# Two items earlier: the order of a grouped hi/lo pipeline in the value half of an expert layer, on one Trainium2 core

## The chip, the cores and the metric

One NeuronCore of one Trainium2 chip runs the whole program in one launch. The metric is the device time of the kernel in microseconds (us), from its runs on the chip. TensorE is named PE in the profile, VectorE DVE, ScalarE ACT, GpSimd POOL, SyncE SP; PEld is TensorE's weight load. The granted clock of TensorE is given as a share of 2.4 GHz.

## The reference, cut to what matters

The program is one step of a hybrid decoder layer: a mixer (SSD and RG-LRU heads), an expert layer with product keys (PEER), and a closing with a per-layer embedding. 544 tokens (512 of a prompt, 8 x 4 decoded) of width 1024 pass through it. The change lies in the expert layer and in preparations for the closing:

```python
u = expert_u[idx]                                            # 16384 experts, 8 heads, top 16
act = jax.nn.gelu(jnp.einsum('td,thkd->thk', tb, u))
v = expert_v[idx]
return jnp.einsum('thk,thkd->td', g * act, v)
...
g = jax.nn.sigmoid(rmsnorm(h, lw['norm_ple_gate']) @ lw['w_ple_gate'])
h = h + rmsnorm((p @ lw['w_ple_proj']) * g, lw['norm_ple_out'])
```

For 384 of the tokens the kernel computes this densely: activations of all 16384 experts (128 blocks of 128), multiplied by a matrix of gates that is zero where an expert was not chosen, times all of expert_v. For the other 160 tokens it gathers the rows of the chosen experts.

## The kernel before, in words

**Stages.** Each engine runs one long program of its own; order between engines comes from semaphores alone. The expert stage (`experts`, from L1424 on) is a loop over 272 items n: n = 0 to 143 (NIT = 144) are the query and U half, n = 144 to 271 (NALL = 272) the V half. V item g = n - 144 (0 to 127) is one block of 128 experts: its slice of expert_v, 128 x 1024, is the weight of 24 matmuls with 384 columns (`v_item`, L1579), three for each of 8 PSUM banks: high weight by high activation (L1587), high weight by low activation (L1588), low weight by high activation (L1589). This splitting of fp32 into a high and a low part in fp32r is done for every operand.

**The ring** (`Ring`, L152 to L170). The weights go through three buffers of four slots. SP loads Rw(m), once ScalarE and VectorE have done with the slot's last item (m - 4); ScalarE rounds it to Rh(m) when TensorE has finished item m - 4; VectorE makes Rl(m) = Rw(m) - Rh(m). Both work four items ahead: at item n they make Rh(n + 4) and Rl(n + 4).

**The groups.** The other operand is made for four items at a time, for group i (items 4i to 4i + 3), in three steps:

- `h_full(i)` (L1958 to L1964, VectorE): Aq = Aq x Gq, the activations times the gates, 128 x 1536. It waits for the loads of Aq(i) and Gq(i // 2).
- `h_hi(i)` (L1720 to L1723, ScalarE): Hh = Aq rounded. It waits for h_full(i) and until TensorE has finished group i - 2, whose buffer it takes.
- `h_lo(i)` (L1966 to L1968, VectorE): Hl = Aq - Hh, counted in semaphore hlo. TensorE waits for it at the group's first item.

Aq has three buffers, Gq, Hh and Hl two each. In each engine's program these steps have fixed places: in VectorE's step for item g with g % 4 = 0 stands h_full(g // 4 + 1), in that with g % 4 = 2 h_lo(g // 4 + 1), in ScalarE's with g % 4 = 1 h_hi(g // 4 + 1). Each step first does the ring's own part, which waits for the end of item g, so that a step runs after its item. Group 0 is made in the last steps of the U half.

**SP's queue** (`sync`, L1460 to L1516). For item m it loads Rw(m). Where m - 151 is 2 modulo 4 it then loads for group i, four groups on, Gq(i // 2) if i is even (`load_g`, L1487, 1.5 MB, waits until h_full has used the buffer) and Aq(i) (`load_a`, L1480, 0.75 MB, waits for `hlo` >= i - 2). A wait on SP holds all loads behind it. All of them use one queue, q1; the gathers of GpSimd use q0.

**The gathered rows** (`row`, L1971; L1976 and L1981). GpSimd gathers 320 times 128 rows of 4 KB (512 KB) into four buffers, at most three ahead of VectorE. VectorE consumes them at a fixed pace, 1.4 per item in the V half, in its step for the item, after the ring's part and the group's.

**First halves of the closing.** `closing` needs the high and low parts of three tensors: the embedding (128 x 1088), its projection (128 x 2048) and the first slice of a gate matrix (128 x 1024). `early_scalar` (L2110 to L2118) rounds all three in a row in ScalarE's step for item 244 (g = 100), `early_vector` (L2120 to L2128) subtracts all three in a row in VectorE's step for item 245. Their loads are issued much earlier (m = 214).

Of the kernel before, what the change touches and what calls it, by code (L numbers as in the profile page):

```python
# [1380 lines left out]
def experts(nc, sh, ring, keys, vn, un, early):  # L1381
# [48 lines left out]
    TURN = 77  # L1430
    G0 = 79
    GEND = 139

    def need(e, name, v):

# [28 lines left out]
    def rows(n):  # L1464

        return range(rows_upto(n - 1), rows_upto(n))
# [200 lines left out]
    def scalar(a):  # L1667
        a.wait_ge(S("sq_free"), 4 * ND)
        a.activation(halves(rstd[:, :]), pair(3), ACT.Sqrt, scale=1.0 / D, bias=sh.epsc[:, 0:1]).then_inc(S("root"), 1)
        a.preload_act_table(ACT.Gelu_apprx_tanh)  # L1670

        def q_out(n, i):
            a.wait_ge(S("wmm"), n + 1)
            need(a, "scm", i - 1)
            a.copy(halves(qT[:, i % 2, :]), pair(1)).then_inc(S("qev"), 1)

        def u_out(n, g):
            if n < NR:
                a.wait_ge(S("evac"), 3 * NXC + g + 1)
                a.activation(Ab[:, g, :], Ab[:, g, :], ACT.Gelu_apprx_tanh).then_inc(S("glu"), 1)  # L1680
                return
            a.wait_ge(S("wmm"), n + 1)
            need(a, "as%d" % (g % 4), 16 * (g // 4))
            a.activation(Ab[:, g % 4, :], PS[:, g % 2, 0:DT], ACT.Gelu_apprx_tanh).then_inc(S("glu"), 1)  # L1684

        def score_out(hd):
            q, r = hd // 4, slice(32 * (hd % 4), 32 * (hd % 4) + 32)
            for s in range(2):
                a.wait_ge(S("scm"), 2 * hd + s + 1)
                need(a, "tkd", hd - 1)  # L1690
                a.copy(tk[:, hd % 2, :, s, :], PS[:, 4 + 2 * s, :].rearrange("p (b k) -> p b k", b=NDB)
                       ).then_inc(S("tkc"), 1)
                a.copy(tkS[r, q, s, :], PS[r, 5 + 2 * s, 0:PK]).then_inc(S("tkc"), 1)

        def turn_out(b):
            a.wait_ge(S("gtp"), b + 1)
            a.copy(ijg[:, :, b * P:(b + 1) * P], PS[:, 4 + b, 0:3 * P].rearrange("p (q t) -> p q t", q=3)
                   ).then_inc(S("gtc"), 1)
            a.mul(ijn[:, b * P:(b + 1) * P], PS[:, 4 + b, 2 * P:3 * P], -2.0).then_inc(S("gtn"), 1)

        def one_hot_act(j):
            t = 4 * j + 3
            a.wait_ge(S("gtc"), t // P + 1)
            a.wait_ge(S("gtn"), t // P + 1)
            need(a, "gmm", j - 3)
            a.activation(Asq[:, j % 2, :], iota[:, :], ACT.Square, scale=-1.0, bias=ijg[:, 0, t:t + 1]
                         ).then_inc(S("gaa"), 1)
            a.wait_ge(S("gaa"), 2 * j + 1)
            a.activation(Aoh[:, j % 4, 3, :], Asq[:, j % 2, :], ACT.Relu, scale=ijn[:, t:t + 1],
                         bias=ijg[:, 2, t:t + 1]).then_inc(S("gaa"), 1)  # L1710

        def gate_out(j):
            b = j // 8
            a.wait_ge(S("gmm"), j + 1)
            if j % 8 == 0 and b >= 2:
                a.wait_ge(S("gw%d" % (b % 2)), 16 * (b // 2))
            a.copy(stg[:, b % 2, :, 4 * (j % 8):4 * (j % 8) + 4].rearrange("p i t -> p t i"),
                   PS[:, 2 + j % 2, :].rearrange("p (t i) -> p t i", t=4)).then_inc(S("gev"), 1)

        def h_hi(i):  # L1720
            a.wait_ge(S("hfd"), i + 1)
            need(a, "wmm", VI + 4 * (i - 1) if i >= 2 else 0)
            a.copy(Hh[:, i % 2, :, :], Aq[:, i % 3, :, :]).then_inc(S("hhi"), 1)  # L1723

        def exps(g):
            a.preload_act_table(ACT.Exp)
            a.wait_ge(S("smx"), g + 1)
            a.activation(tu[:, 4, :], tu[:, 4, :], ACT.Exp).then_inc(S("cf"), 1)
            a.preload_act_table(ACT.Gelu_apprx_tanh)

        a.wait_ge(S("out_s"), 16 * 3)
        for n in range(NIT):
            if n >= NR and u_of(n) is None:
                q_out(n, QITEM.index(n))
            if n >= NR and u_of(n) is not None:
                u_out(n, u_of(n))
            ring.hi(a, n + 4)
            if n < 4:
                for k in (2 * n, 2 * n + 1):
                    a.wait_ge(S("normed"), 2 * ND + k + 1)  # L1740
                    a.copy(Xh[:, k, :], xf[:, k, :]).then_inc(S("xs"), 1)
            if n < NR and u_of(n) is not None:
                u_out(n, u_of(n))
            if n == NR + 2:
                for s, dst in enumerate((xtok, xtokS)):
                    a.wait_ge(S("xt"), s + 1)
                    for q in range(2):
                        a.copy(dst[:, q * 512:(q + 1) * 512], PS[:, 4 + 2 * s + q, :]).then_inc(S("xtc"), 1)
            if head_at(n, 4) is not None:
                score_out(head_at(n, 4))  # L1750
            if n in (LOOK[0] + 1, LOOK[1] + 1):
                exps(LOOK.index(n - 1))
            if n == TURN + 1:
                for b in range(NDB - 1):
                    turn_out(b)
            for j in units(n + 1):
                one_hot_act(j)
            for j in units(n):
                gate_out(j)
            if n == NIT - 1:  # L1760
                h_hi(0)
        for n in range(NIT, NALL):
            if n + 4 < NALL:
                ring.hi(a, n + 4)
            if n == NIT + 100:
                early[1](a)
            g = n - VI
            if g % 4 == 1 and g // 4 + 1 < PK // 4:
                h_hi(g // 4 + 1)
            if rows_upto(n) >= IDC > rows_upto(n - 1):  # L1770
                a.wait_ge(S("sdt"), IDC)
                a.activation(coef[:, :], dots[:, :], ACT.Gelu_apprx_tanh).then_inc(S("cf"), 1)

    def vector(v):
# [183 lines left out]
        def h_full(i):  # L1958
            v.wait_ge(S("aq%d" % (i % 3)), 16 * (i // 3 + 1))
            v.wait_ge(S("gq%d" % ((i // 2) % 2)), 16 * (i // 4 + 1))  # L1960
            v.tensor_tensor(Aq[:, i % 3, :, :].rearrange("p i (b t) -> p i b t", b=NGB),
                            Aq[:, i % 3, :, :].rearrange("p i (b t) -> p i b t", b=NGB),
                            Gq[(i // 2) % 2][:, :, (i % 2) * 4 * GTK:(i % 2 + 1) * 4 * GTK]
                            .rearrange("p b (i t) -> p i b t", i=4), ALU.mult).then_inc(S("hfd"), 1)  # L1964

        def h_lo(i):  # L1966
            v.wait_ge(S("hhi"), i + 1)
            v.tensor_tensor(Hl[:, i % 2, :, :], Aq[:, i % 3, :, :], Hh[:, i % 2, :, :].bitcast(F32), ALU.subtract  # L1968
                            ).then_inc(S("hlo"), 1)
# [15 lines left out]
        for n in range(NALL):  # L1985
# [39 lines left out]
                    one_hot_b(j // 2)  # L2025
                one_hot_a(j)
            g = n - VI
            if n == NIT + 101:
                early[2](v)
            if n == NIT - 2:  # L2030
                h_full(0)
            if n == NIT - 1:
                h_lo(0)
            if g >= 0 and g % 4 == 0 and g // 4 + 1 < PK // 4:
                h_full(g // 4 + 1)
            if g >= 0 and g % 4 == 2 and g // 4 + 1 < PK // 4:
                h_lo(g // 4 + 1)
            for r in rows(n):
                if r == IDC:
                    v.wait_ge(S("cf"), 3)  # L2040
                    v.tensor_tensor(coef[:, :], coef[:, :], gd[:, :], ALU.mult).then_inc(S("cf"), 1)
                    v.wait_ge(S("cf"), 4)
                row(r)
# [11 lines left out]
def closing(nc, sh, pT, w_plg, w_plp, y):  # L2055
# [51 lines left out]
        sp.dma_start(wpr[:, :, :], w_plp).then_inc(S("ple_in"), 16)  # L2107
        sp.dma_start(Wr[0][:, :, :], w_plg[0, :, :, :]).then_inc(S("wp0"), 16)

    def early_scalar(a):  # L2110

        a.wait_ge(S("wmm"), NIT)
        a.wait_ge(S("gmm"), NU)
        a.wait_ge(S("ple_in"), 32)
        a.copy(phi[:, :, :], praw[:, :, :]).then_inc(S("cwhi"), 1)
        a.copy(wph[:, :, :], wpr[:, :, :]).then_inc(S("cwhi"), 1)
        a.wait_ge(S("wp0"), 16)
        a.copy(Wh[0][:, :, :], Wr[0][:, :, :]).then_inc(S("cwhi"), 1)  # L2118

    def early_vector(v):  # L2120

        v.wait_ge(S("cwhi"), 1)
        v.tensor_tensor(plo[:, :, :], praw[:, :, :], phi[:, :, :].bitcast(F32), ALU.subtract).then_inc(S("cwlo"), 1)
        v.wait_ge(S("cwhi"), 2)
        v.tensor_tensor(wpl[:, :, :], wpr[:, :, :], wph[:, :, :].bitcast(F32), ALU.subtract).then_inc(S("cwlo"), 1)
        v.wait_ge(S("cwhi"), 3)
        v.tensor_tensor(Wl[0][:, :, :], Wr[0][:, :, :], Wh[0][:, :, :].bitcast(F32), ALU.subtract
                        ).then_inc(S("cwlo"), 1)  # L2128

    def sync(sp):  # L2130
        sp.wait_ge(S("sdt"), 2 * IDC)
# [357 lines left out]
```

## Time and profile before

| | us |
|---|---|
| median of 3 runs | 1865.39 |
| lowest, highest | 1860.92, 1871.02 |
| profiled execution: span, first to last instruction | 1857.5 |
| lines 1587 to 1589, first to last start (V half) | 1189.6 to 1767.9 |
| TensorE busy in the span | 1774.4 (96%) |
| VectorE busy | 1517.1 (82%) |
| mean granted clock of TensorE | 0.986 |

For the profiled execution the profile gives its span; a time of its own beside the span is not given, and the median of the runs lies 7.9 us above the span. The page of the profile lists busy times of the engines, the costliest groups of instructions and the chain that ended last; the list of waits says which instruction's arrival ended an engine's idle time; windows give busy time, granted clock, DMA share and GB/s of a stretch. Times of instructions are in us from the start of the span.

### The profile page before, as it was taken

How to read it: one execution, taken by the hardware profiler on the slowest of the kernel's cores; microseconds unless marked ns; L12 is line 12 of the kernel's file. 1: busy time of each engine (PE TensorE's matmuls, PEld its weight loads, DVE VectorE, ACT ScalarE, POOL GpSimd, SP SyncE). 2: the span in 40 equal slices, each digit the busy share in tenths (PEclk: the TensorE clock that was granted, in tenths of full speed). 3: DMA queues.
4: the chain of work that ended last, by engine and by line, in shares of the span. 5: the costliest groups of instructions: out<-in, count | busy, mean ns of one | idle time of the engine just before them, and what ended most of it. 6: DMA issues, size and time to landing. Idle time of an engine off the chain costs nothing.

```text
span 1857.5 us, 29685 instructions
## 1 busy us (share of the span) xinstructions
PE 1774.4 (96%) x11346; PEld 1713.3 (92%) x11346; DVE 1517.1 (82%) x2749; ACT 837.9 (45%) x1206; POOL 514.7 (28%) x415
## 2 busy tenths in 40 slices
PE   7999999999999999999999999699999999989996
PEld 6999986789999999999999999699999999989995
DVE  7748896867668689999999989578888888888777
ACT  5556652334334233357777777223333333332263
POOL 3100210000000012344444344344444444444300
PEclk9999999999999999999999999799999999999998
DMA  4222342134335456789999999999999999999511
GB/s 160 83 68 80 132 140 80 63 125 169 123 122 168 169 168 237 264 311 369 366 373 352 362 358 356 379 370 383 368 369 385 388 385 385 371 333 339 204 57 49
DMA packets 164124, 462.82 MB, mean 249 GB/s; under 512 B 16944, under 2 KB 77040, under 8 KB 161296
## 3 DMA queue, kind: packets, MB, share of 16 engines
q1 hardware_dynamic: 117904, 293.13, 44.1%
q0 software_dynamic: 46080, 167.79, 24.1%
q8 instruction: 91, 1.49, 0.3%
q14 instruction: 49, 0.40, 0.1%
HBM read 405.53 MB, written 55.34 MB: 248 GB/s over the span
## 4 chain that ended last, share of the span: by engine, by line
PE 70%; DVE 13%; DMA 11%; ACT 3%; issue 3%; SPq 0%; POOL 0%; DVEq 0%; ACTq 0%
PE PS L470 12%; PE PS L1574 8%; PE PS L1575 8%; PE PS L1576 8%; DMA Rw<-vn 7%; PE PS L1587 5%; PE PS L1589 5%; PE PS L1588 5%; PE PS L1557 5%; PE PS L1644 5%; PE PS L2177 2%; DVE Hl L1968 2%; DMA ug<-vn,idxU 2%; DVE Rl L170 1%; ACT Rh L165 1%
## 5 line engine op out<-in xcount | busy, mean ns | idle before, releaser
L165 ACT CAST Rh<-Rw 128x1024 fp32r<-128x1024 f32 x272 | 284.4, 1046 | 400.8 <-PE PS L1589 338.7
L170 DVE TENSOR_TENSOR Rl<-Rw,Rh 128x1024 fp32r<-128x1024 f32 x272 | 332.5, 1223 | 145.6 <-ACT Rh L165 139.1
L1587 PE MATMUL PS<-Hh,Rh 128*128 128x384 f32 x1024 | 349.4, 341 | 43.7 <-DVE Hl L1968 42.9
L1533 POOL DMA_INDIRECT ug<-un,idxU x160 | 239.3, 1495 | 540.5 <-DVE dots L1976 356.8
L1574 PE MATMUL PS<-Xh,Rh 128*128 128x384 f32 x992 | 342.8, 346 | 3.8 <-DVE Rl L170 2.8
L1589 PE MATMUL PS<-Hh,Rl 128*128 128x384 f32 x1024 | 346.2, 338 | 0.0
L1588 PE MATMUL PS<-Hl,Rh 128*128 128x384 f32 x1024 | 346.0, 338 | 0.0
L1575 PE MATMUL PS<-Xl,Rh 128*128 128x384 f32 x992 | 334.2, 337 | 0.0
L1576 PE MATMUL PS<-Xh,Rl 128*128 128x384 f32 x992 | 333.4, 336 | 0.0
L1533 POOL DMA_INDIRECT ug<-vn,idxU x160 | 230.5, 1441 | 282.3 <-DVE yacc L1981 217.4
L1587 PEld LDWEIGHTS PS<-Hh,Rh 128*128 128x128 f32 x1024 | 195.3, 191 | 53.2 <-issue 53.0
L1588 PEld LDWEIGHTS PS<-Hl,Rh 128*128 128x128 f32 x1024 | 195.3, 191 | 0.0
L1589 PEld LDWEIGHTS PS<-Hh,Rl 128*128 128x128 f32 x1024 | 194.9, 190 | 0.0
L1574 PEld LDWEIGHTS PS<-Xh,Rh 128*128 128x128 f32 x992 | 186.6, 188 | 7.1 <-DVE Rl L170 4.6
L1575 PEld LDWEIGHTS PS<-Xl,Rh 128*128 128x128 f32 x992 | 186.6, 188 | 0.0
L1576 PEld LDWEIGHTS PS<-Xh,Rl 128*128 128x128 f32 x992 | 186.2, 188 | 0.0
L1684 ACT ACTIVATE Ab<-PS 128x384 f32<-128x384 f32 x124 | 60.9, 491 | 255.2 <-PE PS L1576 252.6
L1981 DVE SCALAR_TENSOR_TENSOR yacc<-ug,coef,yacc 128x1024 f32<-128x1024 f32 x128 | 164.6, 1286 | 9.2 <-DMA ug<-vn,idxU 6.0
L1976 DVE CUSTOM_DVE_ANT_0 ug<-ug,xtok 128x1024 f32<-128x1024 f32 x128 | 154.1, 1221 | 19.9 <-DMA ug<-un,idxU 19.6
L470 PE MATMUL PS<-xhi,Whi 128*128 128x272 f32 (+1 forms) x560 | 119.3, 294 | 10.6 <-DVE xlo L913 9.0
L674 ACT CAST Whi<-Wr 128x1024 fp32r<-128x1024 f32 x51 | 53.3, 1044 | 150.6 <-PE PS L470 142.8
L470 PE MATMUL PS<-xhi,Wlo 128*128 128x272 f32 (+1 forms) x560 | 116.6, 290 | 0.0
(438 smaller groups left out, 3150.3 us busy)
## 6 DMA issues: line engine op xcount, KB each, us to landing
Rw<-uw SPq DMA_DIRECT2D x144, 512.0 KB
Rw<-vn SPq DMA_DIRECT2D x128, 512.0 KB
Wr<-wm SPq DMA_DIRECT2D x51, 512.0 KB, 3.3
acts<-Ab SPq DMA_DIRECT2D x128, 192.0 KB
gates<-stg SPq DMA_DIRECT2D x12, 2048.0 KB
Gq<-gates SPq DMA_DIRECT2D x16, 1536.0 KB
Aq<-acts SPq DMA_DIRECT2D x32, 768.0 KB
L<-acsd SPq DMA_DIRECT2D x4, 1024.0 KB, 6.9
```

Of the source, the lines that this page charges most:

```text
L165: a.copy(self.Rh[:, q, :], self.Rw[:, q, :]).then_inc(self.S("rhi"), 1)
L170: v.tensor_tensor(self.Rl[:, q, :], self.Rw[:, q, :], self.Rh[:, q, :].bitcast(F32), ALU.subtract).then_inc(self.S("rlo"), 1)
L470: r = pe.matmul(pair(b, m)[:, q, :], w_sb[:, s, k, 0:m], x_sb[:, k, q * HT:(q + 1) * HT], start=first, stop=last)
L1533: p.indirect_dma_start(out=ug[:, r % 4, :], out_offset=None, in_=un if r < IDC else vn, in_offset=bass.IndirectOffsetOnAxis(ap=idxU[:, r % ...
L1574: pe.matmul(out, Rh[:, q, w], x_hi[:, k, P:NP], start=(k == 0), stop=False)
L1575: pe.matmul(out, Rh[:, q, w], x_lo[:, k, P:NP], start=False, stop=False)
L1576: r = pe.matmul(out, Rl[:, q, w], x_hi[:, k, P:NP], start=False, stop=(k == ND - 1))
L1587: pe.matmul(out, Rh[:, q, w], hh, start=(g == 0), stop=False)
L1588: pe.matmul(out, Rh[:, q, w], hl, start=False, stop=False)
L1589: r = pe.matmul(out, Rl[:, q, w], hh, start=False, stop=(g == PK - 1))
L1976: v.tensor_tensor_reduce(ug[:, q, :], ug[:, q, :], (xtok if own else xtokS)[:, :], 1.0, 0.0, ALU.mult, ALU.add, dots[:, c:c + 1]).then_inc ...
L1981: v.scalar_tensor_tensor(out=y[:, :], in0=ug[:, q, :], scalar=coef[:, c:c + 1], in1=y[:, :], op0=ALU.mult, op1=ALU.add).then_inc(S("sdt"), 1)
```

## The change

Steps of a group move by two items. h_full(i), h_hi(i) and h_lo(i) stand two items earlier in their engines' programs: h_full for group g // 4 + 2 at g % 4 = 2, h_hi for group g // 4 + 2 at g % 4 = 3, h_lo for group g // 4 + 1 at g % 4 = 0. For group 1 this means that h_full(1) runs in VectorE's step for item 142, ahead of h_lo(0), and h_hi(1) right after h_hi(0). The three first halves of the closing are made one by one: on ScalarE in the steps for items 241, 245 and 249, on VectorE in those for 242, 246 and 250. SP's program, TensorE's and GpSimd's are the same.

```diff
+    EARLY = [NIT + 97, NIT + 101, NIT + 105]
...
             if n == NIT - 1:
                 h_hi(0)
+                h_hi(1)
         for n in range(NIT, NALL):
             if n + 4 < NALL:
                 ring.hi(a, n + 4)
-            if n == NIT + 100:
-                early[1](a)
+            if n in EARLY:
+                early[1](a, EARLY.index(n))
             g = n - VI
-            if g % 4 == 1 and g // 4 + 1 < PK // 4:
-                h_hi(g // 4 + 1)
+            if g % 4 == 3 and g // 4 + 2 < PK // 4:
+                h_hi(g // 4 + 2)
...
             g = n - VI
-            if n == NIT + 101:
-                early[2](v)
+            if n - 1 in EARLY:
+                early[2](v, EARLY.index(n - 1))
             if n == NIT - 2:
                 h_full(0)
             if n == NIT - 1:
                 h_lo(0)
             if g >= 0 and g % 4 == 0 and g // 4 + 1 < PK // 4:
-                h_full(g // 4 + 1)
-            if g >= 0 and g % 4 == 2 and g // 4 + 1 < PK // 4:
                 h_lo(g // 4 + 1)
+            if g >= -2 and g % 4 == 2 and g // 4 + 2 < PK // 4:
+                h_full(g // 4 + 2)
...
+    def early_scalar(a, part):
+        if part == 0:
+            a.wait_ge(S("wmm"), NIT)
+            a.wait_ge(S("gmm"), NU)
+            a.wait_ge(S("ple_in"), 32)
+            a.copy(phi[:, :, :], praw[:, :, :]).then_inc(S("cwhi"), 1)
+        elif part == 1:
+            a.copy(wph[:, :, :], wpr[:, :, :]).then_inc(S("cwhi"), 1)
+        else:
+            a.wait_ge(S("wp0"), 16)
+            a.copy(Wh[0][:, :, :], Wr[0][:, :, :]).then_inc(S("cwhi"), 1)
...
+    def early_vector(v, part):
+        v.wait_ge(S("cwhi"), part + 1)
```

`early_vector` is divided in the same way, into its three subtractions.

## Rows read from the trace of the kernel before

**Rows 1.** Page, busy time of the engines, share of the span, instructions.
```profile
PE 1774.4 (96%) x11346; PEld 1713.3 (92%) x11346; DVE 1517.1 (82%) x2749; ACT 837.9 (45%) x1206; POOL 514.7 (28%) x415
```

**Rows 2.** Waits, 1180 to 1775 us: engine, line, releaser; total, times, longest.
```profile
ACT Rh L165 <- DMA Rw<-vn: 45.8, 16, 4.4
PE PS L1587 <- DVE Hl L1968: 42.9, 18, 17.5
...
DVE yacc L1981 <- DMA ug<-vn,idxU: 6.0, 9, 1.2
```

**Rows 3.** Windows by stretch (A, B, C): busy, granted clock, DMA share, GB/s.
```profile
1189.57:1228.09 38.52, 36.26 (x192) 35.67 (x193) 26.61 (x32) 11.20 (x10) 14.25 (x11) 0.93 1.03 381
1228.09:1658.26 430.17, 408.64 (x2304) 401.68 (x2305) 364.73 (x290) 138.07 (x124) 195.21 (x135) 0.99 1.00 375
1658.26:1768.25 109.99, 107.62 (x601) 105.89 (x602) 84.59 (x70) 27.98 (x25) 38.66 (x28) 0.96 0.73 267
```

**Rows 4.** Timeline of DVE and PE around 1422 us; window of items 53 and 54.
```profile
1421.22 1.75 DVE L1968 TENSOR_TENSOR Hl<-Aq,Hh 128x1536 fp32r<-128x1536 f32 x1
...
1422.72 0.34 PE L1589 MATMUL PS<-Hh,Rl 128*128 128x384 f32 x1
1423.12 0.41 PE L1587 MATMUL PS<-Hh,Rh 128*128 128x384 f32 x1
...
1427.36:1435.67 8.31, 8.31 (x49) 8.31 (x49) 6.87 (x6) 3.49 (x3) 2.44 (x2) 1.00 1.05 396
```

**Rows 5.** Chain of waits, 1327 to 1337 us: start, us, what.
```profile
1317.66 14.48 DMA Rw<-vn
...
1332.16 1.06 ACT Rh L165
...
1333.29 1.11 issue
1334.39 1.76 DVE Hl L1968
...
1336.29 0.41 PE PS L1587
```

**Rows 6.** Waits on SP's queue, 1190 to 1770 us.
```profile
SPq L1484 <- DVE Hl L1968: 147.2, 28, 9.1
```

**Rows 7.** Windows with full queues, and of two groups without a listed stall.
```profile
1423.12:1457.07 33.95, 33.80 (x193) 33.22 (x193) 29.77 (x24) 11.19 (x10) 16.08 (x11) 1.00 1.02 383
...
1369.50:1405.50 36.00, 34.35 (x196) 33.53 (x194) 31.20 (x25) 11.19 (x10) 16.23 (x11) 1.00 1.04 394
1477.50:1513.50 36.00, 33.90 (x185) 33.29 (x184) 27.27 (x22) 10.12 (x9) 14.74 (x11) 0.95 1.03 397
1513.50:1549.50 36.00, 34.45 (x196) 33.90 (x197) 31.31 (x25) 12.22 (x11) 16.19 (x11) 1.00 1.02 382
```

**Rows 8.** Timeline of the closing's first halves on DVE, and PE after them.
```profile
1648.10 1.29 DVE L2123 TENSOR_TENSOR ple_lo<-ple_raw,ple_hi 128x1088 fp32r<-128x1088 f32 x1
1649.30 2.29 DVE L2125 TENSOR_TENSOR wp_lo<-wp_raw,wp_hi 128x2048 fp32r<-128x2048 f32 x1
...
1658.26 0.66 PE L1587 MATMUL PS<-Hh,Rh 128*128 128x384 f32 x1 [4.71 <-DVE Hl L1968]
```

**Rows 9.** The entry: chain of waits, timeline of DVE and PE, one window.
```profile
1168.52 14.02 DMA Aq<-acts
...
1182.57 1.76 DVE L1961 TENSOR_TENSOR Aq<-Aq,Gq 128x1536 f32<-128x1536 f32 x1 [9.38 <-DMA Aq<-acts]
...
1189.57 0.66 PE L1587 MATMUL PS<-Hh,Rh 128*128 128x384 f32 x1 [17.51 <-DVE Hl L1968]
...
1182.00:1188.00 6.00, 0.00 (x0) 0.00 (x0) 5.43 (x7) 1.47 (x1) 1.96 (x2) 0.50 1.05 395
```

**Rows 10.** DMA queues from 1210 to 1216 us: packets, MB, share.
```profile
q1 hardware_dynamic: 1680, 1.84, 93.4%
q0 software_dynamic: 97, 0.33, 14.2%
```

More of the change, by code:

```diff
@@ L2108, in early_sync @@
         sp.dma_start(Wr[0][:, :, :], w_plg[0, :, :, :]).then_inc(S("wp0"), 16)
[L2110 to L2128, printed above, removed]
+    def early_scalar(a, part):
[11 more added lines that the diff above has]
+        v.wait_ge(S("cwhi"), part + 1)
+        if part == 0:
+            v.tensor_tensor(plo[:, :, :], praw[:, :, :], phi[:, :, :].bitcast(F32), ALU.subtract
+                            ).then_inc(S("cwlo"), 1)
+        elif part == 1:
+            v.tensor_tensor(wpl[:, :, :], wpr[:, :, :], wph[:, :, :].bitcast(F32), ALU.subtract
+                            ).then_inc(S("cwlo"), 1)
+        else:
+            v.tensor_tensor(Wl[0][:, :, :], Wr[0][:, :, :], Wh[0][:, :, :].bitcast(F32), ALU.subtract
+                            ).then_inc(S("cwlo"), 1)
     def sync(sp):
```

## Prediction

> **What bounds the kernel now.** I read the page first: TensorE is busy for 1774.4 of 1857.5 us [rows 1], so only its own waits can be won. The list of waits says where they lie in the V half: 42.9 us before L1587 on VectorE's Hl, 18 times [rows 2]. The longest, 17.51 us, is the one before V item 0; the other 17 make 25.4 us. The windows by stretch [rows 3] cut the half into A (items 0 to 7, 38.52 us), B (items 8 to 103, 430.17 us) and C (items 104 to 127, 109.99 us).
>
> The reader is to see next that every fourth item waits, even where no stall is listed. In a quiet group Hl runs from 1421.22 for 1.75 us; the last matmul of the item before starts at 1422.72, and its successor not 0.17 us later but at 1423.12, 0.15 us after Hl's end [rows 4]. Inside a group two items take 8.31 us, 4.155 each [rows 4]. So TensorE alone would need 96 x 4.155 = 398.9 us for B, and B takes 31.3 us more.
>
> The chain of waits shows why Hl is late [rows 5]: an Rw load issued at 1317.66 lands after 14.48 us, ScalarE rounds it, VectorE makes Rl, only then comes h_lo in VectorE's order, and TensorE starts at 1336.29, 2.73 us late. In the old order h_lo(i) stands after item 2 of a group and is wanted at the end of item 3. From the end of an item, the hi cast (1.06), Rl (1.11 to its end as the chain shows it) and Hl (1.76) are 3.9 us; with semaphores that is one item, and the slack is nil. SP's queue closes a loop: load_a waits for Hl for 147.2 us in 28 places, 5.3 us each [rows 6], and the ring's loads stand behind it.
>
> The DMA columns say what comes next. Over B the DMA share is already 1.00 at 375 GB/s [rows 3]; the share can pass 1 a little, since packets overlap.
>
> **The change part by part.** No instruction is added or removed. In 31 groups h_full, h_hi and h_lo (1.75 us an Hl [rows 4], and as many elements each) run two items earlier, in the same total of 364.73 us of VectorE in B's 430.17 [rows 3].
>
> *h_lo earlier.* It ends about 4 us after item 0 of the group before and is wanted three items later, 12.5 us: slack 8.5 us in place of none. The largest listed stall inside the loop, 2.73 us, is covered three times. What TensorE waits for next is Rl(m) itself, made four items ahead: three items after its cast may start, so it has about the same 8.5 to 10 us of slack.
>
> *DMAs that move.* load_g stays where it is; it waits only for h_full. load_a(i) is written at the same place but its wait for Hl is now met when SP comes to it, so it goes straight after load_g instead of some 5.3 us later, and the ring's loads behind it are not held. From load_a's issue to h_full(i) there are nine items both before and after. For load_g the distance falls from eleven items to nine, 37 us, against landings of 14 us [rows 5]: covered. The exception is the entry (below).
>
> *h_full and h_hi earlier.* They need Aq and Gq landed, see above. h_hi(i) needs the last item of group i-2 done, which the ring's own cast in the same step already waits for: nothing.
>
> *B: what the freed time is worth.* Here the shares decide. The bytes are fixed: 375 GB/s x 430.17 us = 161.3 MB. At TensorE's 398.9 us that would be 404 GB/s. The three fullest windows of 36 us reached 394, 397 and 382 at shares of 1.02 to 1.04 [rows 7], mean 391. I take 391, as those are windows in which the queues were never empty, which is what the change brings: 161.3 / 0.391 = 412.6 us, a gain of 17.6. Bounds: 383, the rate of two groups that ran without a listed stall [rows 7], gives 421.2 us (gain 9.0); 397 gives 406.3 (gain 23.9). The Trainium skill (HBM Reference, Specifications (TRN2)) gives 358 GB/s as a core's share and about 425 for a core that streams alone. By the first B would take 450 us, more than it does, so the trace refutes it here; by the second B would be TensorE's alone.
>
> *A.* 38.52 us at 381 GB/s is 37.5 at 391: gain 1.0 (0 to 2.6: TensorE alone needs 8 x 4.155 = 33.2 us, and 0.07 x 38.5 = 2.7 for the clock of 0.93 after the entry [rows 3]).
>
> *C, with the closing's first halves.* The three casts and, from 1648.10, the three subtractions each ran in one piece and delayed Hl: 4.71 us of idle TensorE, then matmuls from 0.66 us at its lower level, 1.2 GHz [rows 8]; the granted clock of 0.96 over C is worth 0.04 x 110 = 4.4 us [rows 3]. Now the pieces stand four items apart, the largest 2.29 us on VectorE. In such a step VectorE has Rl 1.1, this 2.3, h_full 1.8 and one or two gathered rows at 1.2 (364.73 us of B less 96 Rl of 1.2 and 48 group steps of 1.75 leave 165 us for 135 gathers [rows 3]): up to 7.6 us against 4.2, hidden by the 8.5 us of slack and by lighter steps around it. Without that cover it would cost 3 us once. C needs 24 x 4.155 = 99.7 us, 10.3 below now; its DMA share is 0.73, so DMA does not bound it as a whole. I take 9, since the last A and G loads fall in its first third (bounds 7, the stall and half of the clock's part, and 10.3).
>
> *The entry.* h_full(1) and h_hi(1) now come before h_lo(0). h_full(0) starts at 1182.57, when Aq(0) has landed after 14.02 us, and TensorE starts at 1189.57, after Hl(0) [rows 9]. h_full(1) puts some 1.7 us between them, and waits for Aq(1), issued right behind. From 1182 to 1188 DMA moved 2.37 MB (6 us at 395 GB/s [rows 9]), three loads of 0.79 MB: Aq(1) landed by 1188 at the latest. Cost 1.7 to 5.5 us; I take 2.7, for one load of 0.79 MB needs 2 us after Aq(0) and VectorE comes to it after 1.7.
>
> **Sum:** -1.0 - 17.6 - 9.0 + 2.7 = -24.9 us against the profiled span of 1857.5, so 1832.6. The median of the runs, 1865.39, lies 7.9 above that span; with it unchanged the forecast is 1840.5 us.
>
> **The rivals.** *TensorE alone bounds it:* -2.6, -31.3, -10.3, +1.7 are -42.5: 1822.9 us. For it: waits for Rw leave 8.5 us of slack. Against: it needs 404 GB/s where the best window shows 397. The skill's 425 GB/s would lead here.
>
> *DMA is already the bound:* the share of 1.00 is saturation, and TensorE's stalls only change their name, from Hl to Rl. For it: 45.8 us of ScalarE's idle time, in 16 places, is on the Rw load [rows 2], and every Rw on the chain takes about 14 us. Then B gives 0 to 9, C 7, the entry costs 4: 3 to 12 us, 1853 to 1862. Against: the mean of B is 1.00 and its fullest window 1.04 [rows 3, 7]; the difference is time in which the queues ran dry.
>
> *Starved gathers (slower):* Gq and Aq now go out as one burst of 2.36 MB, 15 times. While such a burst ran, from 1210 to 1216, queue 1 had 93.4% and the gathers' queue 14.2% [rows 10]. A row that isn't there stops VectorE in row(), and behind it stand the next Rl, h_full and, by rlo, SP's loads. If each burst costs w us that nothing hides, the change is 15 w - 24.9: it decides from w = 1.7, it is slower by over 0.5% from w = 2.3, and at 4 us it is 1900 us. Against: VectorE waits for gathers in all 6.0 us, 1.2 at most [rows 2]. The skill (DMA: Bandwidth & Descriptors, Queues, rings and completion order) says each engine takes turns between queues by packets; by that w would be near 0, and the 14.2% speaks against it.
>
> **Chances.** Forecast 0.58, TensorE alone 0.08, DMA already the bound 0.28, starved gathers 0.06. A measurement here can tell 0.5%, 9.3 us, from no change. The forecast and TensorE's case are faster; of the DMA case's 3 to 12 us a third is over 9.3 us, 0.10. Faster 0.76, same 0.18, slower 0.06. Low end: the forecast's bounds, -2.6 - 23.9 - 10.3 + 1.7 = -35.1, 1830. High end: the forecast's own bad end is 0 - 9.0 - 7 + 5.5 = -10.5, 1855; into the DMA case it reaches 1860, leaving out some 0.2.
>
> **What would show it.** Right: L1587's waits on Hl are gone but for the entry, which is 19 to 21 us; the L1484 waits on SP fall to a few us; B's window shows 385 to 397 GB/s at a share of 1.02 to 1.04 in about 413 us; some TensorE waits reappear before L1587 on Rl (L170); casts and subtractions of the closing lie four items apart and PEclk in C is near 1. Wrong: B at 375 GB/s and Rl waits of 20 us or more (DMA case); items at 4.16 us throughout (TensorE's case); VectorE's waits on ug of 30 us and more (starved gathers).

## The result, and the profile after

The changed kernel takes 1846.47 us (median of 4 runs, 1843.35 to 1850.77), the kernel before 1865.06 beside it; ratio 0.9894, 95% interval 0.9868 to 0.9921. The forecast was 1840.5 us and 24.9 us of gain; it is 18.6 us. The profiled execution (1850.77 us, span 1849.0) is the slowest of its four, and that of before (span 1857.5) lies under the median of its runs, so the two traces differ by 8.5 us only; sizes below are therefore also checked on the other executions with the same order.

The list of waits of the changed kernel, V half (answers to [rows 2]):

```profile
ACT Rh L165 <- DMA Rw<-vn: 229.3, 53, 14.5
...
PE PS L1588 <- DVE Hl L1970: 24.5, 4, 22.7
...
PE PS L1588 <- DVE Rl L170: 15.3, 10, 4.0
...
DVE yacc L1983 <- DMA ug<-vn,idxU: 12.4, 12, 2.1
```

The waits on Hl are gone but for the entry, 22.7 of 24.5 us (the matmul of L1587 is now L1588). In their place TensorE waits for Rl, 10 times, at most 4.0 us; and ScalarE, which waited 45.8 us for Rw loads, now waits 229.3, and 61.9 us for TensorE in place of 338.7. Most of its waiting is now for DMA. Three short waits on Hl are left inside the half, 0.86, 0.86 and 0.16 us.

The windows of the same items A, B and C (C again to the closing's first instruction), for [rows 3]:

```profile
1194.54:1229.58 35.04, 35.04 (x192) 35.04 (x193) 23.57 (x29) 7.70 (x7) 14.90 (x11) 0.95 1.02 376
1229.58:1652.80 423.22, 408.00 (x2306) 403.66 (x2305) 352.63 (x284) 136.07 (x123) 219.19 (x132) 0.99 1.00 374
1652.80:1759.81 107.01, 104.93 (x602) 103.92 (x602) 92.73 (x77) 30.81 (x29) 51.51 (x31) 0.98 0.86 316
```

A gained 3.5 us, B 7.0, C 3.0, and V item 0 starts 5.0 later: 8.5 in all. In B the mean share is 1.00 at 374 GB/s, as before: DMA moved no more per microsecond than it had. It moved less in B (158.3 MB against 161.3, with 132 gathers against 135), and C's share rose from 0.73 to 0.86.

SP's queue and its timeline in the changed kernel (start, us; for [rows 6]):

```profile
SPq L156 <- DVE Rl L170: 362.4, 100, 9.2
...
SPq L1485 <- DVE Hl L1970: 10.9, 1, 10.9
```
```profile
1492.46 0.43 SPq L1490 DMA_DIRECT2D Gq<-gates  x1
1493.06 9.96 SPq L1485 DMA_DIRECT2D Aq<-acts  x1
1503.12 10.56 SPq L158 DMA_DIRECT2D Rw<-vn  x4
1513.86 0.38 SPq L1485 DMA_DIRECT2D Aq<-acts  x1
```

The wait for Hl fell from 147.2 us to one of 10.9 at the entry. But an Aq load issued right behind a Gq load holds SP itself: 9.96 us here, where one without a Gq load in front takes 0.38. The Rw load behind it went out at 1503.12 and landed 13.35 us later, as the chain of waits shows. Behind it h_full, h_lo and the gathered rows stand between the Rl's, which are all late by then, so VectorE catches up slowly:

```profile
1503.12 13.35 DMA Rw<-vn
...
1518.77 1.75 DVE Aq L1963
...
1526.48 1.75 DVE Hl L1970
```

Item by item the trace is plain: items 1 to 32 follow each other at 4.16 us without a gap; then it waits for Rl at items 34, 42, 50, 59, 70, 90, 98, 99, 106 and 107, about once per Gq load, 4.04 us before item 70. The lateness of the Rw loads has eaten the ring's lead by then.

These waits cost TensorE more than their own length. B lies 23.9 us above 96 items of 4.16 us; the listed waits in it sum to 15.1 us. Much of the rest is the low clock behind them: the items behind the waits of 2.54, 4.04 and 2.24 us took 5.86 us or 5.87 each. The window from 1592.24 to 1594.32 lies in such an item, with a granted clock of 0.54; in the next one DMA runs dry:

```profile
1592.24:1594.32 2.08, 2.08 (x8) 2.08 (x8) 1.98 (x2) 2.08 (x2) 0.66 (x1) 0.54 0.97 364
1594.32:1596.40 2.08, 2.08 (x13) 2.08 (x13) 2.08 (x3) 1.28 (x2) 1.77 (x2) 1.00 0.30 89
```

The chain behind that gap: an Rw load issued at 1572.32 landed after 15.88 us, and VectorE stood still for 6.95 us until it could make its Rl at 1589.30. In this time it freed neither a buffer for gathers nor a slot of the ring. GpSimd waited 10.10 us before its gather at 1593.66, and SP issued one Rw load at 1590.60 and the next at 1595.99. So a mean share of 1.00 hides full stretches and gaps. Cut into 101 windows of 4.16 us, one item each, B has 77 with a share of 1.00 or more, which carry 393 GB/s in the mean; the other 24 go down to a share of 0.74 and to 243 GB/s.

### The profile page after: what moved, and what is told of

Its sections match the earlier page's. It is cut to its first block, busy times and chain, and to the rows that moved or that the text cites. A ratio compares the mean times of both kernels' runs of the same rounds, so it can differ in the third digit from the quotient of the medians.

```text
span 1849.0 us, 29685 instructions
## 1 busy us (share of the span) xinstructions
PE 1770.5 (96%) x11346; PEld 1714.0 (93%) x11346; DVE 1511.7 (82%) x2749; ACT 836.2 (45%) x1206; POOL 554.3 (30%) x415
## 4 chain that ended last, share of the span: by engine, by line
PE 68%; DVE 14%; DMA 11%; issue 3%; ACT 2%; SPq 1%; DVEq 0%; ACTq 0%
PE PS L470 12%; DMA Rw<-vn 8%; PE PS L1575 8%; PE PS L1576 8%; PE PS L1577 8%; PE PS L1558 5%; PE PS L1588 5%; PE PS L1589 5%; PE PS L1590 5%; PE PS L1645 5%; PE PS L2185 2%; DVE Rl L170 2%; DVE yacc L1983 2%; DVE ug L1978 1%; SPq L1485 1%
## 5 line engine op out<-in xcount | busy, mean ns | idle before, releaser
L165 ACT CAST Rh<-Rw 128x1024 fp32r<-128x1024 f32 x272 | 282.8, 1045 | 306.6 <-DMA Rw<-vn 229.3
L1588 PE MATMUL PS<-Hh,Rh 128*128 128x384 f32 x1024 | 348.0, 340 | 40.0 <-DVE Hl L1970 24.5
L1534 POOL DMA_INDIRECT ug<-vn,idxU x160 | 267.3, 1671 | 236.2 <-DVE yacc L1983 187.8
L1588 PEld LDWEIGHTS PS<-Hh,Rh 128*128 128x128 f32 x1024 | 194.7, 190 | 45.5 <-issue 26.0
L1983 DVE SCALAR_TENSOR_TENSOR yacc<-ug,coef,yacc 128x1024 f32<-128x1024 f32 x128 | 164.4, 1284 | 15.2 <-DMA ug<-vn,idxU 12.4
L1978 DVE CUSTOM_DVE_ANT_0 ug<-ug,xtok 128x1024 f32<-128x1024 f32 x128 | 153.8, 1219 | 22.7 <-DMA ug<-un,idxU 22.4
```

The lines of the kernel that those rows point to most:

```text
L165: a.copy(self.Rh[:, q, :], self.Rw[:, q, :]).then_inc(self.S("rhi"), 1)
L1534: p.indirect_dma_start(out=ug[:, r % 4, :], out_offset=None, in_=un if r < IDC else vn, in_offset=bass.IndirectOffsetOnAxis(ap=idxU[:, r % ...
L1588: pe.matmul(out, Rh[:, q, w], hh, start=(g == 0), stop=False)
L1978: v.tensor_tensor_reduce(ug[:, q, :], ug[:, q, :], (xtok if own else xtokS)[:, :], 1.0, 0.0, ALU.mult, ALU.add, dots[:, c:c + 1]).then_inc ...
L1983: v.scalar_tensor_tensor(out=y[:, :], in0=ug[:, q, :], scalar=coef[:, c:c + 1], in1=y[:, :], op0=ALU.mult, op1=ALU.add).then_inc(S("sdt"), 1)
```

## The experiments

Twelve kernels, each beside the kernel before on its chip. The last three columns are of each profiled execution: TensorE's wait before V item 0, the time from the start of item 8 to that of item 104, and DMA's rate in it.

| kernel | median us | ratio to before (95%) | entry wait | items 8 to 104 | GB/s, share |
|---|---|---|---|---|---|
| before | 1865.06 | | 17.51 | 430.17 | 375, 1.00 |
| changed | 1846.47 | 0.9894 (0.9868 to 0.9921) | 22.66 | 423.22 | 374, 1.00 |
| e11 h_lo late | 1866.13 | 0.9995 (0.9980 to 1.0010) | 20.64 | 441.17 | 367, 0.99 |
| e3 closing only | 1864.61 | 0.9978 (0.9952 to 1.0004) | 17.21 | 441.87 | 367, 0.98 |
| e2 groups only | 1843.89 | 0.9851 (0.9811 to 0.9892) | 19.98 | 423.30 | 374, 1.00 |
| e1 entry order | 1842.06 | 0.9841 (0.9802 to 0.9880) | 15.65 | 431.12 | 368, 0.99 |
| e7 late load | 1843.59 | 0.9889 (0.9867 to 0.9911) | 20.52 | 414.92 | 381, 1.02 |
| e5 fewer gates, new order | 1818.96 | 0.9757 (0.9736 to 0.9777) | 18.14 | 399.36 | 360, 0.97 |
| e6 fewer gates, old order | 1844.36 | 0.9899 (0.9875 to 0.9924) | 17.47 | 419.95 | 343, 0.93 |
| e4 acts in 6 KB runs | 1834.71 | 0.9804 (0.9764 to 0.9843) | 18.39 | 415.57 | 380, 1.00 |
| e8 acts and gates | 1823.17 | 0.9778 (0.9755 to 0.9801) | 18.60 | 401.58 | 395, 1.00 |
| e10 both layouts, old order | 1846.38 | 0.9903 (0.9878 to 0.9929) | 16.12 | 422.04 | 382, 0.98 |
| e12 early Aq loads | 1827.78 | 0.9798 (0.9779 to 0.9818) | 20.49 | 401.90 | 394, 1.00 |
| e9 best | 1822.83 | 0.9783 (0.9762 to 0.9804) | 18.74 | 399.36 | 397, 1.00 |

**e11: which of the three moves counts.**

```diff
-            if g >= 0 and g % 4 == 0 and g // 4 + 1 < PK // 4:
+            if g >= 0 and g % 4 == 2 and g // 4 + 1 < PK // 4:
                 h_lo(g // 4 + 1)
```

> Changed kernel with h_full and h_hi two items earlier, but h_lo at its old place (item 2 of the group). Theory (h_lo's slack is what the change gives; SP's wait for Hl is back too): waits on Hl at most group starts, 1856 to 1868. Rival (moving the product and the high half brings the gain, by taking h_full out of VectorE's way before Rl): within 3 us of the changed kernel.

The whole gain is gone. Its waits, on TensorE and on SP:

```profile
PE PS L1588 <- DVE Hl L1970: 53.6, 18, 20.6
```
```profile
SPq L1485 <- DVE Hl L1970: 172.2, 29, 10.9
```

18 waits on Hl, as in the kernel before, and SP's wait for Hl is back. Moving the product and the high half is only what makes room for h_lo. Two things come back together here, though: TensorE's waits and SP's. And in e11 h_lo and h_full stand in the same step of VectorE, some 3.5 us in a row, which they do not in the kernel before.

**e2 and e3: groups and closing apart.** In e2 the three parts run in one block at items 244 and 245; in e3 the groups stay where they were.

```diff
 e2, ScalarE (VectorE the same at NIT + 101):
-            if n in EARLY:
-                early[1](a, EARLY.index(n))
+            if n == NIT + 100:
+                for part in range(3):
+                    early[1](a, part)
 e3, VectorE (ScalarE: h_hi back at g % 4 == 1):
-                h_lo(g // 4 + 1)
-            if g >= -2 and g % 4 == 2 and g // 4 + 2 < PK // 4:
-                h_full(g // 4 + 2)
+                h_full(g // 4 + 1)
+            if g >= 0 and g % 4 == 2 and g // 4 + 1 < PK // 4:
+                h_lo(g // 4 + 1)
```

> Groups two items earlier as in the changed kernel, the closing's first halves in one block as before. Theory slack (8 us of slack cover a block of 4.7 us): time as the changed kernel's, 1846 to 1848. Rival (the closing's part carries the gain at items 100 to 104): 5 us or more slower than the changed kernel, 1851 or more, and a TensorE wait of 3 us or more near item 104.

> Groups as before, the closing's first halves four items apart. If the stall of 4.71 us and the low clock behind it (2 us) are the block's: 5 to 7 us faster than before, 1858 to 1860. If DMA is the bound there and gives nothing back: 0 to 2 us faster, 1863 to 1865. Sum check: this gain plus that of the groups alone should make the 18.6 us of the whole, or more than that if they overlap.

The groups alone have all of the gain (1843.89, 2 us under the range expected and not distinguishable from the changed kernel), and there is no TensorE wait at item 104. The closing's move alone is worth 2.8 us against 1867.38 beside it; the interval reaches from 9.0 us faster to 0.7 slower. The block was not the whole cause of the stall of 4.71 us: with the parts four items apart TensorE still waits 3.09 us for Hl before item 104 in e3, and 4.95 us in e11.

**e1: the entry.** h_full(1) stands behind h_lo(0).

```diff
-            if g >= -2 and g % 4 == 2 and g // 4 + 2 < PK // 4:
+            if n == NIT - 1:
+                h_full(1)
+            if g >= 0 and g % 4 == 2 and g // 4 + 2 < PK // 4:
                 h_full(g // 4 + 2)
```

> Changed kernel, but h_full(1) stands behind h_lo(0) on VectorE. Theory DMA (the 16 DMA engines are the bound of the V half's middle, the entry's 5 us are h_full(1) plus its wait for Aq(1)): TensorE's wait before V item 0 falls from 22.7 us by some 2 to 5, to 17.5 to 20.5; of this 0 to 3 us reach the end, so 1843.5 to 1846.5. Rival (the entry's 5 us are the landing of Aq(0) and Gq(0) in that execution, not the order): the wait stays at 21 us or more, the time at 1846.

The wait fell by 7.0 us, more than the 2 to 5 expected and more than h_full(1) can explain, and V item 0 began at 1186.66 instead of 1194.54. Then the window of items 8 to 104:

```profile
1221.49:1652.61 431.12, 407.98 (x2305) 401.86 (x2305) 353.17 (x284) 136.09 (x123) 218.46 (x132) 0.99 0.99 368
```

431.12 us in place of 423.22: it reached item 104 at 1652.61, the changed kernel at 1652.80. An earlier start of 7.9 us was lost again by item 104, at a lower rate and share than in the changed kernel, so a DMA running at a fixed limit does not explain it; TensorE waited for Rl 16 times in the V half, 22.2 us in all. The medians (1842.06 and 1846.47, with overlapping intervals of the ratio) settle no more than that it is not slower.

**e7: SP's order.** Each Aq load from group 4 on waits until TensorE has finished item 3 of its group.

```diff
             need(sp, "hlo", i - 2)
+            if i >= 4:
+                sp.wait_ge(S("wmm"), VI + 4 * (i - 3))
```

> Changed kernel, but SP issues each Aq load (from group 4 on) only when TensorE has finished item 3 of the group, where the wait for Hl held it before the change; the ring's loads behind it are held too. Theory DMA: the order of issue moves no bytes, 0 to 3 us slower than the changed kernel, 1846 to 1849. Rival (the freed SP queue is what brought the gain, the slack of Hl alone little): most of the 18.6 us is lost, 1857 or more.

Nothing is lost. SP now waits 27.3 us for TensorE in 8 places, and its Aq issues still take 55.5 us (67.6 in the changed kernel). So this much holding of SP costs nothing, which speaks for the slack of Hl and against the freed SP queue, a part of my argument. It isn't the full test: the kernel before held SP for 147.2 us there, and what the other 120 us would cost is not shown.

**e5 and e6: DMA's load taken away.** From the third Gq load on only one of twelve blocks is loaded, in the new order (e5) and the old (e6); the gates of those groups are then old ones.

```diff
+            nb = NGB if o < 2 else 1
-            sp.dma_start(Gq[o % 2][:, :, :], gates[:, :, 8 * o:8 * o + 8, :].rearrange("b p i t -> p b (i t)")
+            sp.dma_start(Gq[o % 2][:, 0:nb, :], gates[0:nb, :, 8 * o:8 * o + 8, :].rearrange("b p i t -> p b (i t)")
```

> Changed kernel with the gates loaded whole for groups 0 to 3 alone; for the other 14 loads of Gq only one of 12 blocks is loaded and the rest of the buffer is old, so the result of the expert layer is not the reference's. About 20 of 190 MB of the V half's transfers are left out. Theory DMA: the engines' time bounds items 33 to 110, so without those bytes TensorE runs at 4.16 us per item throughout: item 8 to item 104 in 399 to 402 us (423.2 in the changed kernel), time 1820 to 1826. Rival (the order on VectorE and the ring's depth bound it): item 8 to 104 stays over 412 us, time 1835 or more.

> The kernel before with the same loads of Gq left out, so its result is not the reference's either. If late Rw loads behind Gq and Aq make the stalls on Hl, the long ones go and what is left is the missing slack at each group's start, 0.2 to 0.3 us in 31 groups, and the closing's block: item 8 to 104 in 406 to 412 us, time 1830 to 1840, 8 to 16 us slower than the changed kernel without these loads. If the order itself makes the stalls, it stays above 1850.

The window of items 8 to 104 in e5:

```profile
1225.20:1624.56 399.36, 399.36 (x2306) 399.36 (x2305) 360.63 (x288) 137.66 (x123) 198.77 (x135) 1.00 0.97 360
```

e5 has TensorE busy for all of the 399.36 us, 96 items at 4.16. In the old order 20.6 us are lost even where DMA has room at a share of 0.93: the groups' starts cost some 0.33 us each (items of 4.38 and 4.27 us around them in place of 4.16; 24 of them make 8), and on top of that the stall of 4.71 us before item 104, where the closing's block stands, 4.7, and stalls at five other groups with their low clock the rest, some 8. I had expected 1830 to 1840 and it was 1844.36: I underrated what the old order costs by itself. With fewer bytes to move the new order is worth 25.4 us.

**e4, e8, e10: the same bytes in longer runs.** e4 lays the activations' scratch out so that Aq is one run of 6 KB per partition, e8 also the gates', so that Gq is one run of 12 KB (its stores are then in runs of 1 KB).

```diff
 e4:
-            sp.dma_start(acts[u, :, :], Ab[:, u % 4, :])
+            sp.dma_start(acts[u // 4, :, u % 4 * DT:u % 4 * DT + DT], Ab[:, u % 4, :])
-            sp.dma_start(Aq[:, i % 3, :, :], acts[4 * i:4 * i + 4, :, :].rearrange("i p t -> p i t")
+            sp.dma_start(Aq[:, i % 3, :, :].rearrange("p i t -> p (i t)"), acts[i, :, :]
 e8 besides:
-            sp.dma_start(gates[b, :, :, :], stg[:, b % 2, :, :])
+            sp.dma_start(gates[:, :, b, :].rearrange("o p (i t) -> p o i t", i=8),
+                         stg[:, b % 2, :, :].rearrange("p (o i) t -> p o i t", i=8))
-            sp.dma_start(Gq[o % 2][:, :, :], gates[:, :, 8 * o:8 * o + 8, :].rearrange("b p i t -> p b (i t)")
+            sp.dma_start(Gq[o % 2][:, :, :], gates[o, :, :, :]
```

> Changed kernel, the activations' scratch laid out so that a partition's part of Aq is one run of 6144 bytes in place of four of 1536; same bytes, same order. Theory DMA: the packets' time is the currency of the V half. 1536 bytes took 66 to 72 ns; at the price per byte of the 4096-byte packets (168 ns) they would take 63, so 5 to 12% of a share of 0.13 over 530 us, 3 to 8 us faster than the changed kernel: 1838 to 1843. Rival (latency of the loop Rl, SP, Rw, Rh and VectorE's order, not the engines' time): within 2 us of the changed kernel.

> As the kernel with Aq in runs of 6144 bytes, and the gates' scratch laid out so that a partition's part of Gq is one run of 12 KB in place of twelve of 1 KB; in return the 12 stores of gates write runs of 1 KB in place of 16 KB. Theory DMA: 1 KB packets took 46 to 49 ns, at the price per byte of 4 KB ones 42: 7 to 14% of a share of 0.13 over 430 us, 4 to 8 us faster than with Aq alone (1834.7), less what the stores of 1 KB cost before the V half (2 us at the entry): 1828 to 1834. Rival (writes in runs of 1 KB lengthen the last store, on which the entry waits): 1836 or more, with a longer TensorE wait before V item 0.

> The kernel before with both scratch layouts and nothing else. The layouts took some 23 us from the changed kernel. Theory (the old order stalls at every group's start for want of slack even where DMA has room, as with fewer gates: 1844.4 against 1819.0): 1845 to 1853, so the layouts are worth 13 to 20 us here and the order is worth 22 to 30 us on top, more than the 18.6 us it brought while DMA was the bound. Rival (the two gains add up unchanged): 1842 or less.

Items 8 to 104 in e8 (those of e4 stand in the table):

```profile
1226.63:1628.21 401.58, 399.96 (x2305) 399.29 (x2305) 352.00 (x284) 136.59 (x122) 211.63 (x133) 1.00 1.00 395
```

The mean share stays at 1.00 and the rate rises from 374 to 380 and 395 GB/s; the time falls with it, 7.6 and 21.6 us. In windows of one item with a share of 1.00 or more the rate is 393 GB/s in the changed kernel, 400 in e4 and 406 in e8. The 395 are no limit of DMA: in e8 TensorE is busy for 399.96 of the 401.58 us, so that is what it asked for. e4 beat its expectation (11.8 us under the changed kernel, expected 3 to 8) and so did e8. In e4 SP's issues of Aq behind Gq still take 0.8 to 8.5 us each (28 Aq issues, 75.1 us in sum), so its gain is not a freed SP queue. In e8 they take 0.33:

```profile
1513.19 0.42 SPq L1491 DMA_DIRECT2D Gq<-gates  x1
1513.79 0.33 SPq L1486 DMA_DIRECT2D Aq<-acts  x1
```

So e8 changed two things at once, packets and the held SP queue, and how its further 11.5 us divide between them stays open; e7, where holding SP for 27.3 us cost nothing, speaks for the packets. With the layouts alone (e10) the old order takes 1846.38 us, so the order is worth 23.2 us on top of them.

**e9 and e12: the entry again, with room on DMA.** Both have the layouts, and SP loads Aq(0) to Aq(2) before it waits for the last store of gates; e9 has h_full(1) behind h_lo(0) as well.

```diff
+                for i in range(3):
+                    load_a(i)
                 sp.wait_ge(S("gw0"), 16 * ((NGB + 1) // 2))
                 sp.wait_ge(S("gw1"), 16 * (NGB // 2))
                 load_g(0)
-                for i in range(3):
-                    load_a(i)
```

> Changed kernel with both scratch layouts (Aq in runs of 6 KB, Gq in runs of 12 KB), h_full(1) behind h_lo(0), and at the entry SP loads Aq(0) to Aq(2) before it waits for the last store of gates and loads Gq(0). Theory: with the DMA engines' time no longer the bound (item 8 to 104 was 401.6 us with the layouts, TensorE alone 399.4) a shorter entry now reaches the end in full: 18.6 us of wait before V item 0 fall by the 2 us of h_full(1) and by 2 to 4 us for Aq(0), which no longer lands behind Gq(0): 1817 to 1820. Rival (the entry waits for the store of gates alone, whose landing doesn't change): 1821 to 1824.

> As the best version, but h_full(1) ahead of h_lo(0) as in the changed kernel. Theory: the early loads of Aq give 2 to 4 us against both layouts alone (1823.2), and h_full(1) costs its own 1.7 us at the entry, no wait for Aq(1) any more: 1819 to 1822, 1.7 us above the best version. Rival: no difference from both layouts alone.

A miss. The entry is as long as without it. DVE's timeline of e9 says what it waits for now:

```profile
1184.92 1.76 DVE L1964 TENSOR_TENSOR Aq<-Aq,Gq 128x1536 f32<-128x1536 f32 x1 [12.43 <-DMA Gq<-gates]
```

Gq(0), issued at 1170.76, takes until 1184.9, 14 us, whether Aq(0) goes before it or after. e12, with h_full(1) in front, is 4.9 us above e9 in the median, with intervals that just overlap, and its entry wait 1.75 us longer, h_full(1)'s own time; the early Aq loads bring nothing (e12 is 4.6 us above e8). e9 and e8 are level (1822.83 and 1823.17); e8 is the simpler of the two that beat both kernels, 2.2% under the kernel before.

## Why the prediction was right or wrong

*Sign and mechanism: right.* Waits on Hl end, waits on Rl come in their place, the chain goes through Rw loads of 13 to 17 us. e11 shows that h_lo's place carries the gain. That it does so by TensorE's slack and not by SP's freed queue is shown in part only: e11 brings both back, and e7 holds SP for 27.3 of the 147.2 us. Of the signs named, the waits on Hl and SP's wait went as forecast, the entry's wait was 22.66 us (19 to 21), and B's 385 to 397 GB/s did not come.

*Size: 18.6 us where the sum gave 24.9.* Term by term, with the profiled executions that share an order: old place of h_lo, before, e3 and e11; new, changed, e1, e2 and e7. Their spans differ by 19.4 us in the mean: A 3.8, B 14.6, C 1.6, and V item 0 0.6 later. Against the forecast's 1.0, 17.6, 9.0 and 2.7, C fell short most; that A and the entry came out better by 2.8 and 2.1 hid a part of it, which is luck. These executions differ in other places too, so the means are rough.

- *B, 17.6 us, the step that failed.* The pair of traces gives 7.0; the means over the executions (430.2, 441.9, 441.2 against 423.2, 431.1, 423.3, 414.9) give 437.7 - 423.1 = 14.6. The step is "I take 391, as those are windows in which the queues were never empty, which is what the change brings". The rate is right for full queues: the 77 full windows of one item carry 393 GB/s. But the change does not keep the queues full: 24 of the 101 windows have a share under 1.00, and B as a whole stayed at 374. Nor is a mean share of 1.00 the ceiling: e7 has 1.02 and 381 GB/s over the same items. What the sum left out is the latency of an Rw load behind Gq and Aq, 13 to 17 us on the chain, against a ring four items deep: it stops VectorE, and with it the next loads and gathers. I had given Rl 8.5 to 10 us of slack and not set it against a late load. The rival "DMA is already the bound", to which I gave 0.28, had B's 375 GB/s right, but not its 3 to 12 us, and its Rl waits of 20 us or more were 15.3. Of the windows behind the 391, the one of 397 GB/s holds a load of the closing; why the one of 394 was faster than the others stays open.
- *What DMA gives and takes.* In B the bytes to be moved are not fixed either: the gathers keep to VectorE's pace and spill into C, whose share rose.
- *Entry, 2.7 us.* 5.0 in the pair; V item 0 began at 1189.6 and 1189.8 (before, e3) and at 1194.5, 1192.4 and 1192.4 (changed, e2, e7), 3.4 on the mean, inside the bounds of 1.7 and 5.5. In e5, with the same order at the entry, it began at 1189.6, so the spread between executions is as large as the cost. VectorE did wait for Aq(1), 0.33 us:

```profile
1185.45 1.76 DVE L1963 TENSOR_TENSOR Aq<-Aq,Gq 128x1536 f32<-128x1536 f32 x1 [9.47 <-DMA Aq<-acts]
1187.54 1.76 DVE L1963 TENSOR_TENSOR Aq<-Aq,Gq 128x1536 f32<-128x1536 f32 x1 [0.33 <-DMA Aq<-acts]
```

 The other 2.9 us are the landing of Aq(0), which varies from execution to execution.
- *A, 1.0 us.* 3.5, above its bound of 2.6. TensorE ran this stretch without a gap, for the ring's lead lasted until item 33, and the low clock cost it 1.8 us (item 0 took 5.92) and not the 2.7 of the estimate.
- *C and the closing's parts, 9 us, mis-sized most.* 3.0 in the pair, 108.5 - 106.9 = 1.6 on the means, both under the lower bound of 7. Four errors: the floor of 24 x 4.155 leaves out the last item's transposes (its start to the closing's first instruction is 6.97 us in both traces), and the stall of 4.71 us lies in B, ahead of 1658.26, so I counted it beside B's term. The block alone did not make that stall, as e3 and e11 show. And C itself now has waits for Rl, 0.34 and 1.74 us at items 106 and 107, with an item of 5.88 us behind them. Its DMA share of 0.73 before did not show that. e2 and e3 add that nothing is lost without the move of the closing once Hl has slack, and that by itself it brings 2.8 us, not clear of no change.
- *SP's queue.* "the ring's loads behind it are not held" was wrong: an Aq issue behind a Gq issue holds them for 4.5 us on the mean of 14, the other 14 for 0.38 (all 28 make 67.6 us, 13.5 before). The hold is still smaller than it was, 67.6 us against 147.2 of waiting and 13.5 of issues. e7 shows that 27.3 us more of it did not matter.
- *Starved gathers.* VectorE's wait for yacc's gathers rose from 6.0 to 12.4 us: right in direction, without weight.

## What to carry to other kernels

Two engines that meet once per group need the group's product finished an item or more before its use; with a slack of nil a late load is a stall, and the fix is a place in the order, not speed (e11: the same instructions two items later cost all of the gain). Before costing such a gain, do not read the bound off a mean DMA share. It was 1.00 in B of the changed kernel, where TensorE lost 23.9 us, and 1.00 in that of e9, where it lost nothing. Cut the stretch into windows of one item, look for gaps between full windows, and follow one gap back to the load that was late. Here the rate of the full windows was not reached over the whole stretch, because a buffer ran out while a load waited behind a burst; fewer bytes in the burst (e5) or longer runs (e4, e8) brought that nearer. An experiment that removes bytes tells in one run how much of an order's gain the loads withhold (25.4 us against 18.6 here).

## What the runs showed of the hardware that was not expected

- The same bytes (158 MB) at the same mean share of 1.00: 374 GB/s with runs of 1 and 1.5 KB in Gq and Aq, 380 with 6 KB for Aq, 395 with 12 KB for Gq as well, the last with TensorE as the bound. The Trainium skill (DMA: Bandwidth & Descriptors, Specifications) gives 512 bytes as the least transfer for line rate; by that the layouts would have changed nothing. The measurement decides.
- Stores of gates in runs of 1 KB in place of 16 KB did not lengthen the entry (18.60 us against 18.39 in e4).
- An issue on SP's queue isn't always short: an Aq load (runs of 1.5 KB or of 6 KB) right behind a Gq load in runs of 1 KB took 1.08 to 9.96 us of SP in the changed kernel and 0.77 to 8.49 in e4; behind one in runs of 12 KB 0.33 to 0.36 in e8, and up to 1.37 in e9.
- A single core streamed 397 GB/s over 399 us (e9), above the 358 GB/s that the Trainium skill (HBM Reference, Specifications (TRN2)) gives as a core's share and below the 425 that it gives for a core alone. TensorE did not wait in that stretch, so 397 is what it asked for and not a limit.
